# Attention probabilities scaled by the product that transposes them, in a two-layer hybrid block on one core

## The reference, cut to what matters

```python
def gqa_attend(qblk, k, v):
    s = jnp.einsum('bqgrd,bkgd->bgrqk', qblk, k).astype(jnp.float32) * (HEAD_DIM ** -0.5)
    p = jax.nn.softmax(s, axis=-1).astype(v.dtype)
    return jnp.einsum('bgrqk,bkgd->bqgrd', p, v)
```

## Time and profile before

| | |
|---|---|
| median of 3 runs | 1641.59 us (1641.19 to 1642.63) |
| the profiled execution | 1644.12 us, of which the span of instructions is 1642.3 us |
| busy share of the span | PE 95%, PEld 86%, DVE 54%, ACT 36%, POOL 9% |
| mean granted TensorE clock | 0.984 of full speed |

### The profile page before, as it was taken

One profiled execution on the slowest core, in us unless ns is written; L12 is line 12 of the kernel. 1 busy time (PEld: TensorE's weight loads), 2 busy tenths in 40 slices (PEclk: granted clock), 3 DMA queues, 4 the chain that ended last, 5 costly groups with the idle time before them and its releaser, 6 DMA issues.

```text
span 1642.3 us, 22274 instructions
## 1 busy us (share of the span) xinstructions
PE 1560.3 (95%) x9042; PEld 1406.5 (86%) x9042; DVE 889.1 (54%) x1194; ACT 594.8 (36%) x902; POOL 155.1 (9%) x156
## 2 busy tenths in 40 slices
PE   6999878899999999999999999997899999999999
PEld 4899767699999999999999998996678788888887
DVE  4687775755765554555544367456565433333333
ACT  6634445543622211222112245354545422222223
POOL 0321153001000000000000023014201000000000
PEclk9999999999999999999999999998999999999999
DMA  9555100012353333333331123220003233333322
GB/s 367 165 180 177 40 1 1 1 43 74 103 168 115 128 128 128 117 115 128 128 128 55 49 77 85 65 65 1 1 28 101 77 90 102 90 92 100 90 84 82
DMA packets 203580, 154.74 MB, mean 94 GB/s; under 512 B 8612, under 2 KB 189676, under 8 KB 203372
## 3 DMA queue, kind: packets, MB, share of 16 engines
q1 hardware_dynamic: 202060, 148.85, 29.2%
q10 hardware_dynamic: 1440, 4.78, 0.8%
HBM read 151.52 MB, written 2.10 MB: 94 GB/s over the span
## 4 chain that ended last, share of the span: by engine, by line
PE 82%; DVE 10%; ACT 5%; issue 2%; POOL 0%; DMA 0%; SPq 0%; DVEq 0%; ACTq 0%
PE banks L1734 68%; PE banks L1851 6%; PE banks L2001 1%; DVE neg_max L1549 1%; PE banks L1968 1%; PE banks L1877 1%; PE banks L1945 1%; DVE w_lo L1192 1%; DVE mod_sum L1217 1%; DVE gn_r L1591 1%; DVE nrm L1294 1%; PE banks L1982 1%; DVE h_lo L1288 1%; ACT nrm L860 1%; PE banks L1686 1%
## 5 line engine op out<-in xcount | busy, mean ns | idle before, releaser
L1192 DVE TENSOR_TENSOR w_lo<-raw,w_hi 128x1056 fp32r<-128x1056 f32 x184 | 245.1, 1332 | 305.6 <-ACT w_hi L807 304.8
L1734 PE MATMUL banks<-h_hi,w_hi 128*128 128x384 f32 (+3 forms) x1296 | 387.3, 357 | 16.2 <-DVE h_lo L1288 10.4
L1734 PE MATMUL banks<-h_lo,w_hi 128*128 128x384 f32 (+3 forms) x1296 | 383.9, 354 | 0.0
L1734 PE MATMUL banks<-h_hi,w_lo 128*128 128x384 f32 (+3 forms) x1296 | 383.6, 354 | 0.0
L807 ACT ACTIVATE w_hi<-raw 128x1056 fp32r<-128x1056 f32 x184 | 198.4, 1078 | 255.2 <-PE banks L1734 228.7
L1734 PEld LDWEIGHTS banks<-h_hi,w_hi 128*128 128x128 f32 x1296 | 236.7, 189 | 44.3 <-issue 19.5
L1734 PEld LDWEIGHTS banks<-h_hi,w_lo 128*128 128x128 f32 x1296 | 238.6, 189 | 17.0
L1734 PEld LDWEIGHTS banks<-h_lo,w_hi 128*128 128x128 f32 x1296 | 238.2, 189 | 16.0
L1734 PE MATMUL banks<-g_hi,w_hi 128*128 128x384 f32 (+1 forms) x528 | 160.0, 357 | 0.0
L1734 PE MATMUL banks<-g_hi,w_lo 128*128 128x384 f32 (+1 forms) x528 | 159.1, 355 | 0.0
L1217 DVE SCALAR_TENSOR_TENSOR mod_sum<-mod_ring,cond,mod_sum 128x1024 f32<-128x1024 f32 x126 | 158.1, 1296 | 1.4
(11 more groups left out here) (208 smaller groups left out, 1946.3 us busy)
## 6 DMA issues: line engine op xcount, KB each, us to landing
raw<-in_w_dram SPq DMA_DIRECT2D x120, 512.0 KB, 3.9
mod_ring<-in_w_mod_dram SPq DMA_DIRECT2D x96, 512.0 KB, 4.9
raw<-in_w_in_dram SPq DMA_DIRECT2D x32, 512.0 KB, 5.0
raw<-in_w_out_dram SPq DMA_DIRECT2D x16, 512.0 KB, 3.7
raw<-in_w_dram SPq DMA_DIRECT2D x16, 384.0 KB, 3.2
x_in<-in_x_dram ACTq DMA_DIRECT2D x4, 512.0 KB, 8.1
out_dram<-x_out SPq DMA_DIRECT2D x8, 256.0 KB, 2.3
inv_n<-in_count_dram ACTq DMA_DIRECT2D x4, 400.0 KB, 3.1
```

The source lines that it names most:

```text
L1192: dve.tensor_tensor(w_lo[n % 2][:, :], raw[n % 4][:, :], as_f32(w_hi[n % 2][:, :]), ALU.subtract).then_inc(lo_ready, 1)
L1734: ins = pe.matmul(to(p, a, b), ws[:, w], xs(k, a, b), start=(first and q == 0), stop=(last and q == 2))
```

## The change

The reciprocals are still taken. In place of the multiplication of the probabilities, VectorE multiplies the 128x128 identity by them, which gives a diagonal matrix `p_diag` (two for a context unit, one for each block of queries). TensorE then does not transpose the raw probabilities against the identity, but multiplies them by this diagonal as an ordinary product of float32, which gives the transposed and scaled block in one step. There are three slots for diagonals. Before VectorE overwrites a slot it waits for the products that last read it; those belong to a unit two or three units back.

```diff
@@ -249,6 +249,8 @@
+        p_diag = put("p_diag", [P, 3, P], at=S0 + 23552)
@@ -515,6 +517,16 @@
+        def diag_slot(units, u):
+
+            n = sum(1 + (t < 0) for _, t in units[:u])
+            return [(n + q) % 3 for q in range(1 + (units[u][1] < 0))]
+
+        def diag_last(units, u):
+
+            mine = set(diag_slot(units, u))
+            return max([v for v in range(u) if mine & set(diag_slot(units, v))], default=None)
+
@@ -1462,20 +1474,28 @@
                 def scale_probs(u, t):
 
                     dve.wait_ge(exp_ready, l * INCS["exp_ready"] + u + 1)
-                    if t < 0:
-                        link(dve.reciprocal(p_inv[:, u % 2, 0:2], p_sum[:, u % 2, 0:2]))
-                        for q in range(2):
-                            v = probs[:, u % 3, 256 * q:256 * q + 256]
-                            ins = dve.tensor_scalar(v, v, p_inv[:, u % 2, q:q + 1], None, ALU.mult)
-                        ins.then_inc(p_ready, 1)
-                    else:
-                        link(dve.reciprocal(p_inv[:, u % 2, 0:1], p_sum[:, u % 2, 0:1]))
-                        v = probs[:, u % 3, :]
-                        dve.tensor_scalar(v, v, p_inv[:, u % 2, 0:1], None, ALU.mult).then_inc(p_ready, 1)
+                    slots = diag_slot(units, u)
+                    link(dve.reciprocal(p_inv[:, u % 2, 0:len(slots)], p_sum[:, u % 2, 0:len(slots)]))
+                    last = diag_last(units, u)
+                    if last is not None:
+                        dve.wait_ge(trA, l * INCS["trA"] + trp_job[last][0])
+                        dve.wait_ge(trB, l * INCS["trB"] + trp_job[last][1])
+                    for q, s in enumerate(slots):
+                        ins = dve.tensor_scalar(p_diag[:, s, :], ident, p_inv[:, u % 2, q:q + 1], None, ALU.mult)
+                    ins.then_inc(p_ready, 1)
@@ -1864,7 +1884,7 @@
-                def transposes(jobs):
+                def transposes(jobs, by=None):
@@ -1874,7 +1894,11 @@
-                        ins = pe.transpose(banks[:, bank + k // 4, (k % 4) * P:(k % 4 + 1) * P], src, ident)
+                        dst = banks[:, bank + k // 4, (k % 4) * P:(k % 4 + 1) * P]
+                        if by is None:
+                            ins = pe.transpose(dst, src, ident)
+                        else:
+                            ins = pe.matmul(dst, src, by(k), start=True, stop=True)
@@ -1949,7 +1973,9 @@
-                        transposes([pv[:, k * P:(k + 1) * P] for k in range(4 if t < 0 else 6)])
+                        slots = diag_slot(units, u)
+                        transposes([pv[:, k * P:(k + 1) * P] for k in range(4 if t < 0 else 6)],
+                                   lambda k: p_diag[:, slots[k // 2 if t < 0 else 0], :])
```

More of the change, by code:

```diff
@@ L251, in hybrid_kernel @@
         x_w = put("x_w", [P, 2, 256], at=S0 + 21504)
+        p_diag = put("p_diag", [P, 3, P], at=S0 + 23552)
+        assert S0 + 23552 + 12 * P <= M0 and H0 + 8 * KC * (T + 8) >= S0 + 23552 + 12 * P
         gn_sq = put("gn_sq", [P, T], at=S0 + 9216)
@@ L1464, in _ @@
                 scaled = -1
+                trp_job, jobs_a, jobs_b = {}, 0, 0
+                for e in ev:
+                    if e[0] == "tr":
+                        jobs_a += 1
+                        jobs_b += e[1] != "q" or l < DEPTH - 1
+                    elif e[0] == "trP":
+                        jobs_a += 1
+                        jobs_b += e[2][1] >= 0
+                        trp_job[e[1]] = jobs_a, jobs_b
                 def scale_probs(u, t):
                     dve.wait_ge(exp_ready, l * INCS["exp_ready"] + u + 1)
-                    if t < 0:
-                        link(dve.reciprocal(p_inv[:, u % 2, 0:2], p_sum[:, u % 2, 0:2]))
-                        for q in range(2):
-                            v = probs[:, u % 3, 256 * q:256 * q + 256]
-                            ins = dve.tensor_scalar(v, v, p_inv[:, u % 2, q:q + 1], None, ALU.mult)
-                        ins.then_inc(p_ready, 1)
-                    else:
-                        link(dve.reciprocal(p_inv[:, u % 2, 0:1], p_sum[:, u % 2, 0:1]))
-                        v = probs[:, u % 3, :]
-                        dve.tensor_scalar(v, v, p_inv[:, u % 2, 0:1], None, ALU.mult).then_inc(p_ready, 1)
+                    slots = diag_slot(units, u)
[7 more added lines that the diff above has]
+                    ins.then_inc(p_ready, 1)
                 def y_evac(cc, k):
```

## The result

The changed kernel takes **1653.78 us** (median of 4 executions, 1651.25 to 1656.46) against 1641.39 us of the kernel before: ratio 1.0076, 95% interval 1.0054 to 1.0098, 12.4 us slower. A second set of six executions gave 1653.67 against 1641.34, ratio 1.0077 (1.0061 to 1.0094). The profiled execution took 1651.6 us, with a span of 1649.8 us and a mean granted clock of 0.987.

A forecast was written before the change was run, and what follows sets the result against it. VectorE was taken to bound the passes with `gi`, TensorE the very end, and the blocks or their copies the gated norm. Layer 0's 5.9 and layer 1's 4.3 us summed to +10.2 on 1641.6: 1651.8 us, range 1647 to 1657.

The forecast's parts named there:

- The product costs TensorE twice: Probability blocks on TensorE: two records a block instead of one, 416 for 208; six blocks from 0.65 to 1.30 us.
- The starts: Before the first chunks: +0.44 and +0.40 (0.65 less 0.25 idle) in layer 0, +0.44 in layer 1.
- The chunks gain and lose nothing: Four chunks of layer 0, three of layer 1: 0; added 0.65 fits TensorE's 0.95 us idle, VectorE's saving gains nothing.
- The rows where I said I would be wrong: Blocks have 208 records, the chunk's pass moves over 0.2 us, or the end parts do not become TensorE's.
- Sixth and fourth chunk: Sixth chunk of layer 0: +0.53, VectorE's copy waits for the blocks; fourth of layer 1: +0.65, no idle before it.
- Gated norm, layer 0: Gated norm passes of layer 0: copy late by 0.44, two groups of blocks +0.65 each, four blocks +0.44; sum +2.18.
- Layer 1, from the fourth chunk to the end part: Three gated norm passes of layer 1 where ScalarE's copy directly precedes an exp: 3 x 0.44 = +1.32.
- End parts: Last stretch of each layer: TensorE becomes the bound, gaps of 3.29 and 3.32 close; +2.35 layer 0, +1.88 layer 1.
- The clock rule: If transposes do not count as TensorE activity, the change would save the half-clock spell at layer 0's end: 1650.3 us.
- the "faster" rival: Product costs TensorE one record a block, nothing is added, VectorE's passes with gi save 3.5 us: 1638; chance 0.05.
- four times the cost: All 208 blocks: transpose mode four times faster than the float32 product, 45 us on top, 1697; chance 0.01.
- one spell more or less at each end: Half-clock spell at the two ends, one fewer or one more: 1.5 us either way.

The follow-up runs named there:

- the short GpSimd: GpSimd's three multiplications per chunk cut to 16 columns: in the kernel before, 1640.03 us; together with VectorE making the diagonal and raw probabilities transposed, 1634.7 us.
- D: Against the kernel before, VectorE makes the diagonal instead of scaling, TensorE still transposes the raw probabilities: 1638.97 us, ratio 0.9981.
- e3_float32r: The changed kernel with probabilities and diagonal stored as float32r: 1641.13 us, ratio 0.9997 to the kernel before.
- e2_tensor_part: Against the kernel before, TensorE multiplies the scaled blocks by the identity as a float32 product instead of transposing them: 1656.44 us, ratio 1.008.
- e9_after_again: The changed kernel, unedited, run again beside the kernel before: 1653.67 us, ratio 1.0077.

## Why the prediction was right, point by point

- **The forecast** of slower by 10.2 us, 1651.8 (1647 to 1657), stands against 12.4 us and 1653.8. Direction, mechanism and places hold; the size is 2 us short.
- **The product costs TensorE twice.** Right: 416 records. The term was mis-sized: six blocks take 1.34 us, not 1.30, so a group costs 0.68 more and not 0.65; the pace of 12 records was in the earlier trace rows, and I had taken twice the transposition's start to start instead.
- **The starts.** Predicted 0.44 + 0.40 in layer 0 and 0.44 in layer 1, measured 1.11 and 0.42. The 0.25 us of idle time ahead of the first chunk, which I had subtracted as cover, covers nothing. The start of that piece and its end on TensorE, and then VectorE's copy, read after:

```profile
221.36 1.10 PE L1969 MATMUL banks<-k_T,q_T 128*128 128x512 f32 x2 [1.89 <-ACT probs L1048]
...
231.61 0.71 PE L2027 MATMUL banks<-e_in,x_dt 128*64 128x128 f32 x6 [0.25 <-DVE e_in L1601]
```

```profile
230.53 0.42 DVE L1580 COPY p_T<-banks 128x256 f32<-128x256 f32 x1 [1.22 <-PE banks L1901]
```

  VectorE waits 1.22 us for the blocks, copies them and only then multiplies `e_in`. So the blocks themselves are on the chunk's path here, and the 0.25 us of TensorE are still there.
- **The chunks gain and lose nothing.** Right, -0.02 and -0.03 in four and two intervals; right for the reason given, as the short GpSimd showed. Outside them, VectorE's half gained 0.28 us at the first chunk of layer 1. The rows where I said I would be wrong (the chunk's pass by more than 0.2 us) stayed still.
- **Sixth and fourth chunk**: +0.66 and +0.74, predicted 0.53 and 0.65. The sixth loses nearly its whole group of 0.68.
- **Gated norm, layer 0**: +0.48 (predicted 0.44) and, from norm 1 to the first blocks of the end part, +1.75 (1.74). Layer 1, from the fourth chunk to the end part, 19.24 to 20.56: +1.32 (1.32).
- **End parts.** Predicted +2.35 and +1.88, measured +2.83 (33.14 to 35.97 us from the first blocks to the output projection) and +2.23 (29.47 to 31.70). The gaps closed as forecast: behind 1191.38 no row of TensorE up to 1220.85 has idle time ahead of it. Not all of them were waits for VectorE, as I had written: in the kernel before, 1.37 us of layer 0's 3.29 stand ahead of a `PV` that ScalarE's copy of `mix` (L1056) releases, at 320.85, and 0.33 of layer 1's ahead of 1189.72 likewise. In D the 1.37 shrank to 0.74, so VectorE's passes stand behind a part of it. What was short is the 0.03 us or so a group, 0.3 in each layer, and in layer 0 a little of the spell of half clock, in which the first group now has twice as many records:

```profile
306.07 2.49 PE L1901 MATMUL banks<-p_diag,probs 128*128 128x128 f32 x12 [4.39 <-DVE q_T L1528]
308.35 1.81 PE L1994 MATMUL banks<-p_T,v_tok 128*128 128x256 f32 x4
```

  In this piece of TensorE's timeline after, the group takes 2.28 us against 1.34 at full clock, 0.94 lost where the earlier trace rows lost 0.65. Over the whole spell the difference is only 1.73 against 1.61.
- **The clock rule** of the Trainium skill ("TensorE: Matmul & The Clock Gate", Part 4: PE-mode transpose), by which transposes do not count as activity and the change would save the spell (1650.3): the trace does not bear it out here. The spell comes at the same place, after 4.39 us of idle time of TensorE against 4.46 before, though the blocks ahead of it are now products.
- **A transpose is to be issued as a transpose and not as a standard matmul**, says the Trainium skill ("Perfetto Trace Analysis", Optimizing Tensor Performance, Transposes). The trace agrees, and gives the size, 0.68 us for six blocks of float32.
- **The two rivals by price** are settled by e3_float32r and e2_tensor_part: one record a block would have made the change 2.5 us better at equal clock, where the "faster" rival had 3.5; four times the cost does not occur (416 records, 1.34 us for six blocks).
- **The missing 2 us** of the median: 1.05 are the terms from the first chunks on (9.96 against 8.9) and 0.25 the starts (1.53 against 1.28). The other 0.9 is the mean clock, whose cause is open. Single spells come and go between executions: the first 6 us of layer 0's output projection in the kernel before, the first 2 us of it in the one after, and a row of it in e9_after_again, which is the same changed kernel, read

```profile
334.00:340.00 6.00, 5.47 (x23) 5.50 (x24) 6.00 (x8) 5.62 (x9) 0.00 (x0) 0.72 0.00 0
```

```profile
342.00:344.00 2.00, 1.96 (x11) 1.99 (x12) 2.00 (x3) 2.00 (x4) 0.00 (x0) 1.00 0.00 0
```

```profile
342.38 0.84 PE L1754 MATMUL banks<-m_lo,w_hi 128*128 128x384 f32 x2
```

  Before, the granted clock is 0.72 there, after it is 1.00, so that the 7.5 us by which the output projection began late were 5.9 at 407 us. In e9_after_again the row's two records take 0.84 us where they take 0.51 at full clock: the spell is there again. The prediction allowed for one spell more or less at each end.

## What to carry to other kernels

Before work is moved from one engine to another, ask for each stage which engine ends last, and price the move at that engine: here 0.35 us saved on VectorE was worth 0.35 in ten passes, 0.28 at one chunk and nothing elsewhere, and 0.68 us added on TensorE was free between chunks and paid wherever the blocks, or the copy behind them, stood on the path. Fusing a scaling into a float32 transposition is no saving while it turns one record a block into two. A gain of 0.2% in the stages of a kernel like this one can vanish in the granted clock, so show it in the stage's own marks as well as in the median.

## What the runs showed of the hardware that I had not expected

- The same diagonal product in float32r, one record a block, took 0.73 us for six blocks, near the transposition's 0.66; in float32 it took 1.34.
- Making the 128x128 diagonal takes 0.29 us alone and 0.75 beside GpSimd. The row of 245.55 above ends at 246.30, 0.08 us after GpSimd's `e_cum` (246.22 in its timeline below), where the scaling ended 0.42 us after it. So the small instruction does win there, and the next one beside GpSimd, `e_in`, gives it back. My expectation had put the same 0.4 to 0.6 us behind both.

```profile
244.93 1.29 POOL L775 TENSOR_TENSOR e_cum<-e_cum,c_T 128x512 f32<-128x512 f32 x1
```

- With GpSimd's multiplications cut to 16 columns, all ten `e_in` took 679 to 685 ns, against 680 to 1345 in the changed kernel, with them at full length.
- Eleven of twelve kernels ran at a lower mean clock than before in the same set, by up to 0.0024, which is up to 2 us on the fitted line. Neither why it falls nor why the spell behind 4.4 us of idle time costs 1.36 us in one execution and 3.03 in another does a run here separate.
